# A two-layer mixer trunk on one core: the fourth Strassen sum of h built from the third by two transfers, two weight additions put ahead of the second of them, and the attended rows rounded together

## The chip, the cores and the metric

One Trainium2 chip, one of its cores. The metric is the device time of one execution in microseconds (us). TensorE multiplies matrices, ScalarE (ACT) and VectorE (DVE) do elementwise work, GpSimd (POOL) starts the transfers that add while they write, and SyncE (SP) starts the plain transfers of weights.

## The reference: what is computed

```python
for l in range(2):                                    # DEPTH = 2, x is 512 x 1024
    h = rms_norm(x, norm_g[l])
    proj = einsum('bsd,de->bse', h, w_in[l])          # columns: a_u a_v a_z b_q b_k b_v b_z i_q i_k i_w g_a g_b
    y_a = spatial_gating_branch(gelu(a_u), gelu(a_v), a_z, ...)
    att = sparse_attention_branch(q, k, v, qi, ki, i_w, topk=128)   # 4 heads x 128, keys chosen by an indexer
    y_b = att * silu(b_z)
    o_a = einsum('bse,ed->bsd', y_a, w_oa[l])
    o_b = einsum('bse,ed->bsd', y_b, w_ob[l])
    merged = sigmoid(g_a + gate_b[l, 0]) * o_a + sigmoid(g_b + gate_b[l, 1]) * o_b
    x = x + einsum('bsd,de->bse', merged, w_out[l])
```

All is float32.

## The kernel before

Every matrix product is made of three passes. Each operand is kept as a rounded part (`_hi`, type fp32r) and the rest (`_lo`), and three matmuls add hi times lo, lo times hi and hi times hi. ScalarE writes each hi (a Copy that rounds), VectorE each lo (a subtraction). A weight piece, a **unit**, is 256 rows by 512 columns (512 KB): it lands in one of four slots of `w_raw`, ScalarE rounds it (L1065), VectorE writes the rest (L1427), and the slot is free again.

The work of a layer is a fixed list of **jobs** on TensorE, in this order: iq, k, q, vb, va, u, zb, za (4 jobs each), ga (14), oa (8), gb (14), ob (8), out (14). Four jobs are called ZA0 to ZA3 here, and so on. Every engine walks through the same job numbers in a program written by hand. For job n ScalarE rounds the units that a table gives to n, empties the bank, and then does what stands "beside" the job: attention steps, sums. TensorE does an attention step (scores of step i, transposes of step i-1, weighted values of step i-2; L851, L842, L833) after ZA2 and then after GA0, GA2, GA4 and so on.

The ga, gb and out products use Strassen's scheme (in Winograd's form) on two by two blocks: seven products, each of two jobs, in the order a11 (GA0, GA1), a12 (GA2, GA3), s5 (GA4, GA5), s3 (GA6, GA7), s6 (GA8, GA9), s4 (GA10, GA11), a22 (GA12, GA13). Here a11, a12, a21 and a22 are the blocks of h transposed (upper or lower half of the channels, left or right half of the tokens), and the s are sums of them:

- s5 = a21 - a22, s3 = a21 - a22 - a11, s6 = a12 + a21 - a22 - a11, s4 = a21 - a11 (a sign apart).

The sums of h are made without VectorE: ScalarE copies one part into a buffer (`h_part_copied`, L1186), and POOL starts transfers that add further parts to it in place (`add_term`, L711). Each block has a hi and a lo part, so each is two terms. s5 is summed in `h5_raw`, s3 in `h3_raw`, s6 in `h6_raw`, and s4 in the lower token half of `g_a`, which is free only once the mixing matmuls before ZA1 are done; `h_beside` holds the lo part of -a11 meanwhile. `h_sum_rounded` (L1173) then rounds a sum on ScalarE, beside ZA3 (s5), GA0 (s3), GA2 (s6) and GA4 (s4), and `h_sum_remainder` (L1567) writes its rest on VectorE. Rounding s5 writes over a21, where it stood in h.

The weights of s5, s3, s4 and a22 are sums too. POOL adds a block of the weights to what a slot of `w_raw` still holds (`add_weights`, L737), once the rest of that slot's unit is written. In ga these are the units 4 and 5 (s5), 8 and 9 (s3), 10 and 11 (s4), 12 and 13 (a22). POOL issues all of it in the order of its program, and a wait there holds back what stands behind it. Units 6 and 7 (s6) are plain transfers by SP. ScalarE rounds units 4 and 5 at GA0, 6 and 7 at GA2, 8 at GA3, 9 at GA4, 10 at GA6.

After attention, `z_b` holds the attended rows times their gate, four heads of 128 channels. ScalarE rounds each to `yb_hi` (L1311), VectorE writes `yb_lo` (L1711), both at the jobs of `SPLIT_YB`. The first job of ob, OB0, uses them head by head. When all four are there, POOL reloads x into `x_sb` (L748), which the out jobs need.

Of the kernel before, what the change touches and what calls it, by code (L numbers as in the profile page):

```python
# [184 lines left out]
_slots = JOB_ZA[2:3] + JOB_GA[::2] + JOB_OA[::2] + JOB_GB[0:11:2]  # L185
AFTER_ATT = {_slots[i]: i for i in range(len(ATT_STEPS) + 2)}

SPLIT_YB = {JOB_GB[11]: [0, 1], JOB_GB[12]: [2], JOB_GB[13]: [3]}
assert min(SPLIT_YB) > max(AFTER_ATT)

X_AFTER = {2: [1], 4: [2], 5: [3]}

ROUNDS = TOPK // 8
H_PARTS = ["-a22 hi to s5", "-a22 lo beside", "a12 hi to s6", "-a11 hi to s3", "-a11 lo beside", "-a11 hi to s4"]
H_PARTS_AFTER = {JOB_VB[2]: 0, JOB_VB[3]: 1, JOB_VA[0]: 2, JOB_VA[1]: 3, JOB_VA[3]: 4, JOB_ZA[1]: 5}
H_TERMS = {"s5": 3, "s3": 2, "s6": 2, "s4": 3}
H_SIGN = {"s5": -1.0, "s3": 1.0, "s6": -1.0, "s4": -1.0}
H_HI_AFTER = {JOB_ZA[3]: "s5", JOB_GA[0]: "s3", JOB_GA[2]: "s6", JOB_GA[4]: "s4"}
H_LO_AFTER = {JOB_GA[1]: "s5", JOB_GA[3]: "s3", JOB_GA[5]: "s6", JOB_GA[7]: "s4"}
# [47 lines left out]
def trunk(nc, x, norm_g, w_in, gate_b, a_ln_g, a_ln_b, a_ws, a_bs, q_norm_g, k_norm_g, w_oa, w_ob, w_out,  # L247
          ident, rope_cs, out):
    ctx = ExitStack()
    with ctx:  # L250
# [298 lines left out]
        def top(tile, k=slice(0, HALF_K)):  # L549
            return tile[:, k, 0:SEQ // 2]  # L550

        def bottom(tile, k=slice(0, HALF_K)):
            return tile[:, k, SEQ // 2:SEQ]
# [89 lines left out]
        def _(pool):  # L643
# [6 lines left out]
            for layer in range(DEPTH):  # L650
# [56 lines left out]
                def add_term(name, n, src):  # L707

                    if n > 0:
                        pool.wait_ge(s_hterm[name].sem, s_hterm[name].at(layer, 16 * n))  # L710
                    pool.dma_start(h_sum_raw(name), src, accum_op=ALU.add).then_inc(s_hterm[name].sem, 16)  # L711

                def part_copied(part):
                    pool.wait_ge(s_hpart.sem, s_hpart.at(layer, H_PARTS.index(part) + 1))

# [10 lines left out]
                add_term("s3", 1, h_sum_raw("s5"))  # L726
                pool.wait_ge(s_hterm["s3"].sem, s_hterm["s3"].at(layer, 32))
                add_term("s6", 1, h_sum_raw("s3"))
                part_copied("-a11 hi to s4")
                add_term("s4", 0, h_beside[:])  # L730
                add_term("s4", 1, a21_hi)
                add_term("s4", 2, a21_lo)

                def add_weights(u):
                    slot = raw_slot(layer, u)
# [4 lines left out]
                for g in (GA_G, GB_G):  # L740
                    for u in range(UNIT_FIRST[g], UNIT_FIRST[g] + SEVEN):
                        if unit_adds(u):
                            add_weights(u)

                pool.wait_ge(s_yblo.sem, s_yblo.at(layer, HEADS))
                pool.wait_ge(s_stash.sem, s_stash.at(layer, 16))
# [304 lines left out]
        def _(act):  # L1051
# [108 lines left out]
            def h_sum_rounded(layer, name):  # L1160
                act.wait_ge(s_hterm[name].sem, s_hterm[name].at(layer, 16 * H_TERMS[name]))
                if name == "s5":
                    act.wait_ge(s_job.sem, s_job.at(layer, JOB_ZA[-1] + 1))
                    act.wait_ge(s_hterm["s4"].sem, s_hterm["s4"].at(layer, 48))
                    act.wait_ge(s_hterm["s3"].sem, s_hterm["s3"].at(layer, 32))
                if name == "s3":
                    act.wait_ge(s_hterm["s6"].sem, s_hterm["s6"].at(layer, 32))
                    act.wait_ge(s_hterm["s4"].sem, s_hterm["s4"].at(layer, 16))
                if name == "s6":
                    act.wait_ge(s_hslo.sem, s_hslo.at(layer, H_ROUNDED.index("s5") + 1))  # L1170
                if name == "s4":
                    act.wait_ge(s_ya.sem, s_ya.at(layer, A_GROUPS))
                nc.scalar.activation(gate_operand(name)[0], h_sum_raw(name), ACT.Copy,  # L1173
                                     scale=H_SIGN[name]).then_inc(s_hshi.sem, 1)

            def h_part_copied(layer, i):

                f, upper = (lambda block: block.bitcast(F32)), slice(HALF_K, KD)
                if H_PARTS[i] == "-a11 lo beside":
                    act.wait_ge(s_hterm["s5"].sem, s_hterm["s5"].at(layer, 16))  # L1180
                if H_PARTS[i] == "-a11 hi to s4":
                    act.wait_ge(s_mix.sem, s_mix.at(layer, A_GROUPS))
                dst, src, sign = [(h_sum_raw("s5"), f(bottom(h_hi, upper)), -1.0), (h_beside[:], f(bottom(h_lo, upper)), -1.0),
                                  (h_sum_raw("s6"), f(top(h_hi, upper)), 1.0), (h_sum_raw("s3"), f(top(h_hi)), -1.0),
                                  (h_beside[:], f(top(h_lo)), -1.0), (h_sum_raw("s4"), f(top(h_hi)), -1.0)][i]
                nc.scalar.activation(dst, src, ACT.Copy, scale=sign).then_inc(s_hpart.sem, 1)  # L1186

            def evacuate(layer, n):
# [79 lines left out]
            def beside(layer, n):  # L1268

                for i in AFTER_IDX.get(n, []):  # L1270
                    b, h = IDX_STEPS[i]
                    w = P * (b + 1)
                    act.wait_ge(s_idxp.sem, s_idxp.at(layer, i + 1))

                    if i >= 2:
                        act.wait_ge(s_idx.sem, s_idx.at(layer, i - 1))
                    nc.scalar.activation(probs[:, i % 2, 0:w], bank[3 + i % 2][:, 0:w], ACT.Relu).then_inc(s_relu.sem, 1)
                if n == AFTER_WS:
                    act.wait_ge(s_wst.sem, s_wst.at(layer, 1))
                    four = bank[5][:].rearrange("p (c q) -> p c q", c=A_GROUPS)  # L1280
                    act_.mark(nc.scalar.activation(ws_t[0:CHUNK], four[0:CHUNK], ACT.Copy))
                    act_.mark(nc.scalar.activation(ws_t[CHUNK:P, :, CHUNK:P], four[CHUNK:P, :, CHUNK:P], ACT.Copy))
                    act_.join(act)
                    act.sem_inc(s_wsc.sem, 1)
                if n - 1 in JOB_ZA:
                    c = n - 1 - JOB_ZA[0]
                    act.wait_ge(s_ya.sem, s_ya.at(layer, c + 1))
                    nc.scalar.activation(ya_hi[:, c], u_a[:, c], ACT.Copy).then_inc(s_yahi.sem, 1)
                if n in AFTER_ATT:
                    i = AFTER_ATT[n]  # L1290
                    if i >= 1 and i <= len(ATT_STEPS):
                        b = ATT_STEPS[i - 1][1]
                        w = P * (b + 1)
                        act.wait_ge(s_pt.sem, s_pt.at(layer, i))
                        if i >= 2:
                            act.wait_ge(s_pv.sem, s_pv.at(layer, i - 1))
                        nc.scalar.activation(probs_t[:, 0:w], bank[5][:, 0:w], ACT.Copy).then_inc(s_ptc.sem, 1)
                    if i < len(ATT_STEPS):
                        w = P * (ATT_STEPS[i][1] + 1)
                        act.wait_ge(s_max.sem, s_max.at(layer, i + 1))  # L1300
                        act_.mark(nc.scalar.activation(probs[:, i % 2, 0:w], probs[:, i % 2, 0:w], ACT.Exp,
                                                       bias=neg_max[:, i:i + 1], scale=ATT_SCALE,
                                                       accum_out=row_sum[:, i:i + 1]))
                        act_.join(act)
                        act.sem_inc(s_exp.sem, 1)
                        act.wait_ge(s_rowinv.sem, s_rowinv.at(layer, i + 1))
                        nc.scalar.activation(probs[:, i % 2, 0:w], probs[:, i % 2, 0:w], ACT.Copy,
                                             scale=row_inv[:, i:i + 1]).then_inc(s_prob.sem, 1)
                for h in SPLIT_YB.get(n, []):
                    act.wait_ge(s_yb.sem, s_yb.at(layer, TILES))  # L1310
                    nc.scalar.activation(yb_hi[:, h], z_b[:, h], ACT.Copy).then_inc(s_ybhi.sem, 1)  # L1311
                if n in H_PARTS_AFTER:
                    h_part_copied(layer, H_PARTS_AFTER[n])
                if n in H_HI_AFTER:
                    h_sum_rounded(layer, H_HI_AFTER[n])
                if n in JOB_OB:
                    d = n - JOB_OB[0]
                    if d == 0:
                        act.wait_ge(s_job.sem, s_job.at(layer, JOB_GB[-1] + 1))
                    if d == KD - 1:  # L1320
                        s5_rounded(layer, 0)
                        rounded(layer, OUT_U + 4)
                    if d % 2:
                        merged_hi(layer, d // 2)
                    if d == KD - 1:
                        s5_rounded(layer, 1)
                if n == JOB_OUT[2]:
                    sum_rounded(layer, "s6")
                if n == JOB_OUT[3]:
                    sum_rounded(layer, "s3")  # L1330
                if n == JOB_OUT[7]:
                    sum_rounded(layer, "s4")
                if n == JOB_OUT[8]:
                    bottom_hi(layer)
# [507 lines left out]
```

## Time and profile before

| what | value |
| --- | --- |
| time, median of 3 runs | 815.54 us (814.4 to 815.74) |
| time of the profiled execution | 814.92 us |
| its span | 813.1 us |
| TensorE busy | 776.1 us (95% of the span) |
| VectorE busy | 627.1 us (77%) |
| ScalarE busy | 429.0 us (53%) |
| POOL busy | 172.1 us (21%) |
| mean busy share of the DMA engines by POOL's queue, by SP's | 32.7%, 24.7% |

Busy time is time in which an engine executes something; start times are us from the start of the span. The span is 1.8 us shorter than the device time of the same execution. The two layers run one after the other: the first reaches GA0 at about 210 us, the second at about 608 us.

### The profile page before, as it was taken

To read this page: it belongs to the slowest core of one execution; us is meant where nothing else is said; L and a number is where in the kernel's file an instruction comes from. 1 tells how busy PE (TensorE), PEld (TensorE's weight loads), DVE (VectorE), ACT (ScalarE), POOL (GpSimd) and SP (SyncE) were. 2 spreads that over 40 slices of the span, in tenths; PEclk is the share of its full clock that TensorE was granted. 3 is DMA by queue.
4 is the path that set the end of the run, shared out by engine and by line. 5 is a ranking of instruction groups with operands and counts; after the bars stand their busy time and mean duration, and the time that the engine had idled before them with its cause. 6 is when DMAs were issued, how large, how long until landed. Compare 5 with 4: busy or idle time off the path is not lost.

```text
span 813.1 us, 12210 instructions
## 1 busy us (share of the span) xinstructions
PE 776.1 (95%) x4412; PEld 679.3 (84%) x4412; DVE 627.1 (77%) x1050; ACT 429.0 (53%) x790; POOL 172.1 (21%) x153
## 2 busy tenths in 40 slices
PE   7999999999769999999999999999994999999998
PEld 6988888888769889988899888888884998899886
DVE  5779999978278775669886899997962887746895
ACT  6576555343267546744564765544243764577242
POOL 1157501100220003012211664110012201110130
PEclk9999999999979999999999999999997999999999
DMA  9544237821976437676873531576247854476774
GB/s 335 201 128 132 61 112 165 199 60 53 165 120 159 127 79 130 184 212 136 185 230 104 168 107 61 128 163 177 79 91 116 133 178 78 96 123 197 207 135 125
DMA packets 55597, 114.72 MB, mean 141 GB/s; under 512 B 3568, under 2 KB 9904, under 8 KB 55536
## 3 DMA queue, kind: packets, MB, share of 16 engines
q0 software_dynamic: 24016, 48.32, 32.7%
q1 hardware_dynamic: 31232, 65.02, 24.7%
q8 instruction: 35, 0.57, 0.3%
q10 hardware_dynamic: 288, 0.59, 0.2%
q14 instruction: 26, 0.21, 0.1%
HBM read 97.14 MB, written 6.29 MB: 127 GB/s over the span
## 4 chain that ended last, share of the span: by engine, by line
PE 75%; DVE 9%; DMA 7%; issue 5%; ACT 3%; POOL 1%; ACTq 0%; DVEq 0%; SPq 0%; POOLq 0%
PE bank L859 15%; PE bank L861 15%; PE bank L860 15%; PE bank L980 4%; PE bank L927 4%; PE bank L929 4%; PE bank L928 4%; DVE w_lo L1427 3%; PE bank L833 2%; PE bank L896 2%; PE bank L898 2%; PE bank L897 2%; PE bank L851 2%; DMA g_a<-h_beside 2%; DMA g_a<-h_hi 1%
## 5 line engine op out<-in xcount | busy, mean ns | idle before, releaser
L1427 DVE TENSOR_TENSOR w_lo<-w_raw,w_hi 128x1024 fp32r<-128x1024 f32 x156 | 201.4, 1302 | 34.5 <-ACT w_hi L1065 30.5
L1065 ACT ACTIVATE w_hi<-w_raw 128x1024 fp32r<-128x1024 f32 x156 | 160.4, 1052 | 30.7 <-DMA w_raw<-in_w_out 16.6
L859 PE MATMUL bank<-w_lo,h_hi 128*128 128x512 f32 x256 | 100.5, 393 | 0.0
L861 PE MATMUL bank<-w_hi,h_hi 128*128 128x512 f32 x256 | 99.9, 390 | 0.0
L860 PE MATMUL bank<-w_hi,h_lo 128*128 128x512 f32 x256 | 99.8, 390 | 0.0
L927 PE MATMUL bank<-h_hi,w_lo 128*128 128x256 f32 x256 | 77.8, 304 | 2.0 <-DVEq L1581 2.0
L737 POOL DMA_DIRECT2D w_raw<-in_w_in x32 | 39.7, 1241 | 181.1 <-DVE w_lo L1427 173.7
L859 PE MATMUL bank<-h_lo,w_hi 128*128 128x512 f32 x192 | 75.2, 392 | 0.0
L861 PE MATMUL bank<-h_hi,w_hi 128*128 128x512 f32 x192 | 74.7, 389 | 0.0
L860 PE MATMUL bank<-h_hi,w_lo 128*128 128x512 f32 x192 | 74.7, 389 | 0.0
L928 PE MATMUL bank<-h_lo,w_hi 128*128 128x256 f32 x256 | 74.0, 289 | 0.0
L929 PE MATMUL bank<-h_hi,w_hi 128*128 128x256 f32 x256 | 73.9, 289 | 0.0
L927 PE MATMUL bank<-hs,w_lo 128*128 128x256 f32 x192 | 56.5, 294 | 2.7 <-DVE w_lo L1427 2.7
L1496 DVE MAX8 top<-score 128x8 f32<-128x256 f32 (+2 forms) x96 | 53.5, 558 | 5.5 <-DVE g_a L1629 2.6
L861 PEld LDWEIGHTS bank<-w_hi,h_hi 128*128 128x128 f32 x256 | 48.1, 188 | 10.3
L859 PEld LDWEIGHTS bank<-w_lo,h_hi 128*128 128x128 f32 x256 | 48.1, 188 | 9.3
L860 PEld LDWEIGHTS bank<-w_hi,h_lo 128*128 128x128 f32 x256 | 48.1, 188 | 9.3
L927 PEld LDWEIGHTS bank<-h_hi,w_lo 128*128 128x128 f32 x256 | 50.9, 199 | 4.1 <-DVEq L1581 2.4
L929 PE MATMUL bank<-hs,w_hi 128*128 128x256 f32 x192 | 53.8, 280 | 0.0
L928 PE MATMUL bank<-hs,w_hi 128*128 128x256 f32 x192 | 53.8, 280 | 0.0
L928 PEld LDWEIGHTS bank<-h_lo,w_hi 128*128 128x128 f32 x256 | 50.8, 199 | 1.6 <-issue 1.4
L1497 DVE MATCH_REPLACE8 score<-top,score 128x256 f32<-128x256 f32 (+2 forms) x96 | 52.1, 542 | 0.0
(209 smaller groups left out, 1862.7 us busy)
## 6 DMA issues: line engine op xcount, KB each, us to landing
w_raw<-in_w_in SPq DMA_DIRECT2D x88, 512.0 KB, 4.5
w_raw<-in_w_in POOLq DMA_DIRECT2D x32, 512.0 KB, 6.0
w_raw<-in_w_out POOLq DMA_DIRECT2D x16, 512.0 KB, 7.5
w_raw<-in_w_out SPq DMA_DIRECT2D x12, 512.0 KB, 4.1
out<-x_sb POOLq DMA_DIRECT2D x4, 1024.0 KB, 5.5
w_raw<-in_w_oa SPq DMA_DIRECT2D x8, 512.0 KB, 3.4
w_raw<-in_w_ob SPq DMA_DIRECT2D x8, 512.0 KB, 4.2
x_sb<-out POOLq DMA_DIRECT2D x2, 2048.0 KB, 8.9
```

The source lines that it names most:

```text
L737: pool.dma_start(w_raw[:, slot], block_weights(layer, u), accum_op=ALU.add) \
L859: nc.tensor.matmul(dst, s_h, m_l, start=(n == 0), stop=False)
L860: nc.tensor.matmul(dst, s_l, m_h, start=False, stop=False)
L861: last = nc.tensor.matmul(dst, s_h, m_h, start=False, stop=(n == len(pairs) - 1))
L927: nc.tensor.matmul(dst, w_lo[:, wk, col], a_hi[:, k], start=first and i == 0, stop=False, skip_group_check=True)
L928: nc.tensor.matmul(dst, w_hi[:, wk, col], a_lo[:, k], start=False, stop=False, skip_group_check=True)
L929: last = nc.tensor.matmul(dst, w_hi[:, wk, col], a_hi[:, k], start=False, stop=(k == HALF_K - 1), skip_group_check=True)
L980: last = nc.tensor.matmul(dst[:, 0:width], h[:, k, tok], w[:, k, first:first + width], start=(k == 0 and n == 0), stop=(k == KD - 1 and n ...
L1065: nc.scalar.activation(hi, w_raw[:, raw_slot(layer, u)], ACT.Copy).then_inc(s_whi.sem, 1)
L1427: nc.vector.tensor_tensor(lo, w_raw[:, raw_slot(layer, u)], hi.bitcast(F32), ALU.subtract) \
L1496: vec.link(dve, nc.vector.max(top8[:], s))
L1497: vec.link(dve, nc.vector.match_replace(s, top8[:], s, TAKEN))
```

## The change

s4 now starts from a22 (its hi part copied by ScalarE) and gets two terms: the finished sum s3 from `h3_raw`, and the lo part of a22. It had three, the lo part of -a11, and both parts of a21. The second term is started only after the weight additions of units 4 and 5. ScalarE, before it rounds s5, no longer waits for the terms of s4; before it rounds s3 it still waits for the first of them. And the attended rows are rounded at one place (GB11) in place of three, their rests are written at two places in place of three.

```diff
-SPLIT_YB = {JOB_GB[11]: [0, 1], JOB_GB[12]: [2], JOB_GB[13]: [3]}
+SPLIT_YB = {JOB_GB[11]: [0, 1], JOB_GB[12]: [2, 3]}
...
-H_PARTS = ["-a22 hi to s5", "-a22 lo beside", "a12 hi to s6", "-a11 hi to s3", "-a11 lo beside", "-a11 hi to s4"]
+H_PARTS = ["-a22 hi to s5", "-a22 lo beside", "a12 hi to s6", "-a11 hi to s3", "-a11 lo beside", "a22 hi to s4"]
...
-H_TERMS = {"s5": 3, "s3": 2, "s6": 2, "s4": 3}
+H_TERMS = {"s5": 3, "s3": 2, "s6": 2, "s4": 2}
...
-                part_copied("-a11 hi to s4")
-                add_term("s4", 0, h_beside[:])
-                add_term("s4", 1, a21_hi)
-                add_term("s4", 2, a21_lo)
+                part_copied("a22 hi to s4")
+                add_term("s4", 0, h_sum_raw("s3"))
...
                         if unit_adds(u):
                             add_weights(u)
+                        if u == UNIT_FIRST[GA_G] + 5:
+                            add_term("s4", 1, bottom(h_lo, slice(HALF_K, KD)).bitcast(F32))
...
                 if name == "s5":
                     act.wait_ge(s_job.sem, s_job.at(layer, JOB_ZA[-1] + 1))
-                    act.wait_ge(s_hterm["s4"].sem, s_hterm["s4"].at(layer, 48))
                     act.wait_ge(s_hterm["s3"].sem, s_hterm["s3"].at(layer, 32))
...
-                                  (h_beside[:], f(top(h_lo)), -1.0), (h_sum_raw("s4"), f(top(h_hi)), -1.0)][i]
+                                  (h_beside[:], f(top(h_lo)), -1.0), (h_sum_raw("s4"), f(bottom(h_hi, upper)), 1.0)][i]
...
-                for h in SPLIT_YB.get(n, []):
+                for h in range(HEADS if n == min(SPLIT_YB) else 0):
                     act.wait_ge(s_yb.sem, s_yb.at(layer, TILES))
                     nc.scalar.activation(yb_hi[:, h], z_b[:, h], ACT.Copy).then_inc(s_ybhi.sem, 1)
```

On POOL, this is the place of each layer between the sums of h and the weight additions of ga (`w_raw<-in_w_in` are those additions, the first two of them units 4 and 5; the sixteen are those of ga and gb):

```order
 L711 DMA h_raw<-h_lo 128x4x256
 L711 DMA h_raw<-h_raw 128x1024 x2
-L711 DMA g_a<-h_beside 128x4x256
-L711 DMA g_a<-h_hi 128x4x256
+L711 DMA g_a<-h_raw 128x4x256
+L735 DMA w_raw<-in_w_in 128x2x512 x2
 L711 DMA g_a<-h_lo 128x4x256
-L737 DMA w_raw<-in_w_in 128x2x512 x16
+L735 DMA w_raw<-in_w_in 128x2x512 x14
```

Units 4 and 5 stood behind three terms of s4 and now stand behind one; the last term has moved behind them, ahead of unit 8.

On ScalarE, this is the end of gb in the first layer, from the gates of GB10 on, before the change (L1134 are tanh of the gates, L1065 rounds weights):

```order
L1065 ACTIVATE w_hi<-w_raw 128x1024
L1134 ACTIVATE g_b<-g_b,gate_half 128x256 x2
L1311 ACTIVATE yb_hi<-z_b 128x512 x2
L1134 ACTIVATE g_b<-g_b,gate_half 128x256 x2
L1134 ACTIVATE g_b<-bank,gate_half 128x256 x2
L1311 ACTIVATE yb_hi<-z_b 128x512
L1134 ACTIVATE g_b<-bank,gate_half 128x256 x2
L1311 ACTIVATE yb_hi<-z_b 128x512
```

and of the changed kernel:

```order
L1065 ACTIVATE w_hi<-w_raw 128x1024
L1134 ACTIVATE g_b<-g_b,gate_half 128x256 x2
L1310 ACTIVATE yb_hi<-z_b 128x512 x4
L1134 ACTIVATE g_b<-g_b,gate_half 128x256 x2
L1134 ACTIVATE g_b<-bank,gate_half 128x256 x4
```

The third and the fourth rounding have moved ahead of the gates of s4 and a22.

## Rows read from the trace of the kernel before

**Rows 1.** Waits of TensorE by releaser: us in total, times, longest us.

```profile
PE bank L833 <- ACT probs_t L1297: 19.1, 2, 9.8
PE bank L842 <- ACT probs L1307: 2.7, 2, 1.4
...
PE bank L859 <- DVE yb_lo L1711: 1.0, 2, 0.5
```

**Rows 2.** Windows, first layer: length, busy (instructions) by engine, TensorE clock, DMA, GB/s.

```profile
209.80:218.90 9.10, 9.10 (x76) 8.91 (x74) 2.08 (x3) 1.12 (x2) 2.50 (x2) 1.00 0.83 117
218.90:228.20 9.30, 0.02 (x1) 0.00 (x0) 1.41 (x2) 4.34 (x6) 2.41 (x2) 0.62 0.83 128
...
230.90:234.70 3.80, 3.80 (x20) 3.80 (x20) 3.73 (x6) 2.90 (x5) 1.22 (x1) 0.50 0.39 47
234.70:242.90 8.20, 7.45 (x61) 7.18 (x60) 6.90 (x14) 6.02 (x12) 2.42 (x2) 1.00 0.99 154
```

**Rows 3.** Timeline of ScalarE: start us, us, line, what, [idle before <-releaser].

```profile
210.50 0.62 ACT L1288 ACTIVATE ya_hi<-u_a 128x512 fp32r<-128x512 f32 x1
219.84 1.06 ACT L1173 ACTIVATE h_hi<-h_raw 128x1024 fp32r<-128x1024 f32 x1 [8.72 <-DMA g_a<-h_lo]
222.37 1.06 ACT L1065 ACTIVATE w_hi<-w_raw 128x1024 fp32r<-128x1024 f32 x1 [1.47 <-DMA w_raw<-in_w_in]
225.93 1.06 ACT L1065 ACTIVATE w_hi<-w_raw 128x1024 fp32r<-128x1024 f32 x1 [2.50 <-DMA w_raw<-in_w_in]
...
227.88 0.27 ACT L1297 ACTIVATE probs_t<-bank 128x128 f32<-128x128 f32 x1
```

**Rows 4.** Timeline of POOL: when it issues its transfers.

```profile
201.27 1.31 POOL L711 DMA_DIRECT2D g_a<-h_beside  x1 [41.24 <-ACT g_a L1186]
...
213.77 1.28 POOL L711 DMA_DIRECT2D g_a<-h_lo  x1 [4.47 <-DMA g_a<-h_hi]
214.52 1.75 POOL L737 DMA_DIRECT2D w_raw<-in_w_in  x1
220.05 1.21 POOL L737 DMA_DIRECT2D w_raw<-in_w_in  x1 [3.78 <-issue]
```

**Rows 5.** The chain that ended last, two transfers: start us, us to landing.

```profile
201.27 6.22 DMA g_a<-h_beside
...
220.05 5.86 DMA w_raw<-in_w_in
```

**Rows 6.** Transfers issued at 214.52 us: KB, us to landing.

```profile
w_raw<-in_w_in POOLq DMA_DIRECT2D x1, 512.0 KB, 7.8
```

**Rows 7.** Timeline of VectorE, first layer.

```profile
229.79 1.21 DVE L1427 TENSOR_TENSOR w_lo<-w_raw,w_hi 128x1024 fp32r<-128x1024 f32 x1
...
232.42 1.22 DVE L1567 SCALAR_TENSOR_TENSOR h_lo<-h_raw,h_hi 128x1024 fp32r<-128x1024 f32 x1
...
241.61 1.22 DVE L1427 TENSOR_TENSOR w_lo<-w_raw,w_hi 128x1024 fp32r<-128x1024 f32 x1
```

**Rows 8.** Timeline of TensorE, the first matmul of GA6.

```profile
242.97 0.36 PE L927 MATMUL bank<-hs,w_lo 128*128 128x256 f32 x1 [0.82 <-DVE w_lo L1427]
```

**Rows 9.** Unit 8: when POOL issues it and ScalarE rounds it.

```profile
224.99 1.20 POOL L737 DMA_DIRECT2D w_raw<-in_w_in  x1 [3.74 <-DVE w_lo L1427]
```

```profile
238.29 1.04 ACT L1065 ACTIVATE w_hi<-w_raw 128x1024 fp32r<-128x1024 f32 x1
```

**Rows 10.** Second layer: the first term of s4 in the chain, and unit 5 on ScalarE.

```profile
599.59 6.21 DMA g_a<-h_beside
```

```profile
624.75 1.06 ACT L1065 ACTIVATE w_hi<-w_raw 128x1024 fp32r<-128x1024 f32 x1 [2.40 <-DMA w_raw<-in_w_in]
```

**Rows 11.** Timeline of ScalarE at the end of gb, first layer.

```profile
343.27 1.15 ACT L1311 ACTIVATE yb_hi<-z_b 128x512 fp32r<-128x512 f32 x2
...
351.29 0.63 ACT L1311 ACTIVATE yb_hi<-z_b 128x512 fp32r<-128x512 f32 x1 [0.19 <-ACT g_b L1134]
```

**Rows 12.** Timeline of TensorE in OB0, the fourth head's first product.

```profile
352.80 0.47 PE L859 MATMUL bank<-yb_lo,w_hi 128*128 128x512 f32 x1 [0.51 <-DVE yb_lo L1711]
```

More of the change, by code:

```diff
@@ L1180, in h_part_copied @@
                     act.wait_ge(s_hterm["s5"].sem, s_hterm["s5"].at(layer, 16))
-                if H_PARTS[i] == "-a11 hi to s4":
+                if H_PARTS[i] == "a22 hi to s4":
                     act.wait_ge(s_mix.sem, s_mix.at(layer, A_GROUPS))
```

## The prediction

> **What bounds the kernel now.** I read the waits of TensorE first, since it is busy 95% of the span and only its idle time or a slow clock can be won back quickly. The reader is to see that one line holds most of it: 19.1 us in two waits, for ScalarE's copy of the transposed probabilities, and 2.7 us more in two waits for the scaled probabilities [rows 1]. Next the windows around the first of these: TensorE ends GA2 at 218.9 us, stands until 228.2, and comes back at half its clock (0.50 granted, 1.2 of 2.4 GHz) until 234.7; three jobs took 9.10 us before that, so a ga job is 3.0 us [rows 2]. Third, ScalarE's timeline: it is idle too. It ends the third `ya_hi` at 211.12, then waits 8.72 us for the last term of s4 before it may round s5 at 219.84, then for unit 4 (222.37), then for unit 5 (225.93); only after those comes the copy that TensorE waits for, at 227.88 [rows 3]. Fourth, POOL: the three terms of s4 go out one after the other, each once the former has landed, at 201.27 and 213.77 for the first and the last, and units 4 and 5 queue behind them, at 214.52 and 220.05 [rows 4]. So the stall is made of two things in one line: a rounding (s5) that waits for a sum needed much later (s4, used at GA10), and two weight additions needed now (GA0 rounds them) that are issued behind that sum.
>
> From unit 5 on, the pace is VectorE's, not TensorE's: the rest of unit 5 is written at 229.79, that of s5 at 232.42, that of unit 8 at 241.61 [rows 7], and TensorE, though it came 9 us late and at half clock, waits again at 242.97 for that last one [rows 8]. So what this place can win is the time by which ScalarE gets unit 5 earlier. The slow clock is not a gain to be added: it lies inside the shadow of VectorE's chain.
>
> **The change, part by part.**
>
> *ScalarE's rounding of s5.* It no longer waits for s4. Its other conditions hold: TensorE ended ZA3 at 210, before the `ya_hi` of 210.50 [rows 3], s5 and s3 were complete before the part for s4 was copied, since POOL had only that part left to wait for at 201.27 [rows 4]. It starts where the third `ya_hi` ends, 211.1, and takes 1.06 [rows 3], so ScalarE can take unit 4 at 212.1 and unit 5 at 213.1 if they have landed.
>
> *POOL.* One transfer of 512 KB a layer is gone. The first term leaves at 201.27 as before and lands 6.22 us later, at 207.5 [rows 4, 5]; its source is another buffer of the same size, which I cost at nothing. Unit 4 may follow at 202.6, since its slot is free long before (POOL issued it right behind a term before too, at 214.52, with no idle time ahead [rows 4]). Two transfers in flight share the engines: the term issued at 213.77 had landed when ScalarE started at 219.84, unit 4 landed at 214.52 + 7.8 = 222.3, so 2.6 us behind, and unit 5 at 220.05 + 5.86 = 225.9, 3.6 us behind unit 4 [rows 3 to 6]. So unit 4 now lands at 210.1 to 211.1, ahead of 212.1. Unit 5 was issued 3.78 us after unit 4 with nothing shown that it waited for, and just as the term ahead of both had landed [rows 4]. I take it that the queue holds two of these and no third. Then unit 5 now leaves at about 207.8 and lands at 213.7 (5.86 later) if it runs as it did, or at 214.7 (3.6 behind unit 4) if the engines are shared. I take the middle, 214.2. ScalarE then has it 225.93 - 214.2 = **11.7 us** earlier. Upper bound: ScalarE's own 213.1, a gain of 12.8. Lower bound: 214.7 and the 0.5 us by which SP's units 6 and 7, in flight at the same time, might push it, a gain of 10.7.
>
> On transfers that add, a rule and the trace differ. The row gives 5.86 us for 512 KB [rows 5]. The Trainium skill, DMA: Bandwidth & Descriptors, section on the anatomy of one DMA on the GpSimd path, gives 2.0 us plus the bytes at 436 GB/s, an estimate of 3.2 us for this size. By it unit 5 would land at 211 and the gain would be the upper bound, 12.8. The trace does not agree, so the row decides.
>
> *The second layer.* From the first term to unit 5 on ScalarE it is 624.75 - 599.59 = 25.16 us, against 24.66 in the first [rows 3, 4, 10], with a first term that takes the same 6.21. The gain is 0.5 more: **12.2 us**, upper bound 13.3.
>
> *What is late next.* Everything that hung on unit 5 shifts by 11.7. The rest of s5 is done at 232.42 + 1.22 - 11.7 = 221.9; TensorE no longer stands after GA2 (the copy it wants comes at 227.88 - 11.7 = 216.2), does the attention step and GA3, and reaches GA4 at 222.2: no wait to speak of. It reaches GA6 two jobs and an attention step later, at 228.6, and the rest of unit 8 is there at 241.61 + 1.22 - 11.7 = 231.1. So the wait at GA6 grows from 0.82 [rows 8] to about 2.5 us. It is inside the 11.7: GA6 starts at 231.3 against 242.97.
>
> *The moved term.* The last term of s4 is issued behind unit 5 once there is room, about 211, and ahead of unit 8. It lands at about 218; s4 is rounded beside GA4, after unit 8, so not before 226. Unit 8 waits for the rest of unit 4 (about 214.3) and for room, leaves at about 214.5 and lands at 220.5 to 222. ScalarE wants it at 238.29 - 11.7 = 226.6 [rows 9]. So the moved term costs nothing, with 4.5 to 6 us in hand. Unit 9 is issued when the rest of unit 5 is written, which shifts with it.
>
> *ScalarE's copy for s4* reads another block of the same size: nothing.
>
> *The attended rows.* OB0 waited 0.51 us for the fourth head's rest [rows 12], because ScalarE rounded that head only behind the gates of a22, at 351.29 [rows 11]. Now the four roundings run from 343.27, two of them took 1.15, so the last ends at 345.6. That covers the gates of s4 by some 0.2 us, where ScalarE next waits for TensorE's a22, so nothing. The last rest is written at GB12, about 349, before OB0 wants it. A gain of 0.5 us a layer; the waits for it are 1.0 us in all [rows 1]: **1.0 us**. The reload of x starts some 4 us earlier and nothing waits for it before OUT0.
>
> **Sum.** 11.7 + 12.2 + 1.0 = 24.9 us. The profiled execution took 814.92 us (span 813.1), so it would take 790.0 (span 788.2). The median shown is 0.6 above it; I predict 790.6 for the median.
>
> **The rivals.**
>
> *Unit 5 is there before ScalarE asks.* If the pause of 3.78 us was no lack of room, three transfers run at 2.6 us apart: 207.5, 210.1, 212.7, before 213.1. Gains 12.8 + 13.3 + 1.0 = 27.1, time 788.4. Against it: the pause, in both layers. Chance 0.12. By the page DMA: Bandwidth & Descriptors of the Trainium skill (above) it would be the same time.
>
> *The transfers do not overlap here.* SP's units 6 and 7 run at the same time, and if unit 4 lands a whole 5.9 us behind the term and unit 5 another 5.9 behind that, it is 219.3, gains 6.6 + 7.1 + 1.0 = 14.7, time 800.8. Against it the 2.6 and 3.6 of the trace. Chance 0.07.
>
> *The clock.* The low clock took 7.1 us of the stall (a mean of 0.62 over 9.30 us) and lasted to 234.7, 13.6 us in all [rows 2]. Now TensorE has a wait of 2.5 us at GA6. Were the clock to fall on that, TensorE would work through such a stretch itself, at 0.19 us a matmul (3.80 us for 20) in place of 0.12 (9.10 us for 76): some 5 us a layer, time 801. Against it: after the 0.82 us wait the window shows 1.00. Chance 0.05. The Trainium skill, TensorE: Matmul & The Clock Gate, section on oscillation, tells of a kernel in which repeated waits for transfers kept the engine on the low clock; no row here shows that without a stall of 9 us.
>
> *Slower: the moved term holds unit 8.* POOL stands at the second term of s4 until the first has landed and there is room, and units 8 to 13 stand behind it. Past the 4.5 to 6 us in hand every us comes off the gain, and it decides at 11.7 + 6, some 18 us late: then the kernel is slower (each further 1 us costs 2, say 820 at 20 us late). Nothing in the trace takes 18 us. Chance 0.02. That something else holds ScalarE at the same place, so that nothing changes, has 0.02.
>
> **How the numbers follow.** Forecast 0.72, own range 789 to 793; ceiling 0.12 (788.4); no overlap 0.07 (800.8); clock 0.05 (801); slower 0.02; no change 0.02. A range of 787.5 to 797 takes the first two and partly overlapping or partly slowed cases. A change of 0.2%, 1.6 us, is about what can be told from none. Faster 0.96, same 0.02, slower 0.02.
>
> **What would show it.** TensorE's wait for `probs_t` (19.1 us) gone, and no low clock near 230 and 630. ScalarE rounding s5 at 211.1 without a wait, unit 4 at 212.1 without one, and unit 5 after about 1 us of waiting, at 214.2. POOL issuing at 201.3, 202.6, 207.8, then the term near 211. A wait of about 2.5 us at GA6 for `w_lo`. OB0 without a wait for `yb_lo`. Unit 8 not waited for by ScalarE. The prediction is wrong if unit 5 comes after 216, or if the low clock shows up again.

## The result, and the profile after

The changed kernel takes 793.58 us (median of 4 runs, 792.18 to 795.45) against 814.97 us before in the same comparison. The ratio is 0.9739, 95% interval 0.9715 to 0.9763: 21.4 us less, where 24.9 were forecast. The profiled execution took 792.18 us, span 790.4, and is the fastest of the four.

The waits of TensorE in the changed kernel (us in total, times, longest us), against [rows 1]:

```profile
PE bank L927 <- DVEq L1582: 3.6, 2, 1.8
PE bank L842 <- ACT probs L1306: 3.1, 2, 1.7
...
PE bank L927 <- DVEq L1580: 2.0, 2, 1.0
...
PE bank L927 <- DVE w_lo L1426: 1.4, 2, 0.8
```

The 19.1 us for `probs_t` are gone, and so is the wait for `yb_lo`. New is a wait of 1.8 us in each layer on something that VectorE released at L1582. ScalarE in the first layer, against [rows 3]:

```profile
210.33 1.05 ACT L1172 ACTIVATE h_hi<-h_raw 128x1024 fp32r<-128x1024 f32 x1
212.55 1.06 ACT L1065 ACTIVATE w_hi<-w_raw 128x1024 fp32r<-128x1024 f32 x1 [1.17 <-DMA w_raw<-in_w_in]
215.42 1.06 ACT L1065 ACTIVATE w_hi<-w_raw 128x1024 fp32r<-128x1024 f32 x1 [1.81 <-DMA w_raw<-in_w_in]
...
217.38 0.27 ACT L1296 ACTIVATE probs_t<-bank 128x128 f32<-128x128 f32 x1
```

It rounds s5 at once and then waits twice for weights, in all 3 us. POOL's issues, against [rows 4]:

```profile
200.59 1.31 POOL L711 DMA_DIRECT2D g_a<-h_raw  x1 [41.69 <-ACT g_a L1185]
201.34 3.03 POOL L735 DMA_DIRECT2D w_raw<-in_w_in  x2
207.38 1.30 POOL L711 DMA_DIRECT2D g_a<-h_lo  x1 [3.01 <-DMA g_a<-h_raw]
215.22 1.19 POOL L735 DMA_DIRECT2D w_raw<-in_w_in  x1 [6.54 <-DVE w_lo L1426]
```

Units 4 and 5 leave one right behind the other while the first term is in flight (x2, 201.34 to 204.37): there is no pause between them. Windows, to be read as [rows 2] (length, busy of TensorE, its weight loads, VectorE, ScalarE, POOL, then the clock):

```profile
209.10:218.20 9.10, 9.10 (x78) 9.08 (x76) 3.98 (x6) 5.35 (x8) 1.19 (x1) 1.00 1.15 218
...
222.20:226.00 3.80, 1.99 (x17) 1.78 (x16) 3.15 (x6) 1.33 (x3) 1.24 (x2) 1.00 0.86 134
226.00:230.00 4.00, 4.00 (x23) 4.00 (x22) 3.35 (x7) 3.55 (x8) 1.22 (x1) 0.57 0.95 140
230.00:234.00 4.00, 4.00 (x36) 4.00 (x36) 3.36 (x7) 3.37 (x9) 1.21 (x1) 1.00 0.81 130
```

The long low clock is gone. A short one stands in the first layer behind two waits, one of 1.4 us for `probs`, as before the change, and the new one of 1.8 us: 23 matmuls in 4 us in place of 36.

To compare kernels without the scatter at their start, I measure one stretch in each trace: from ScalarE's tanh of ZA3 (210.00 before, 209.32 after) to the end of the last wait of TensorE in ga, which every variant has. Before and after these are:

```profile
264.73 0.39 PE L927 MATMUL bank<-h_hi,w_lo 128*128 128x256 f32 x1 [0.99 <-DVEq L1581]
```

```profile
254.24 0.38 PE L927 MATMUL bank<-h_hi,w_lo 128*128 128x256 f32 x1 [0.98 <-DVEq L1580]
```

So the **ga stretch** of the first layer took 264.73 - 210.00 = 54.7 us before and 254.24 - 209.32 = 44.9 after: 9.8 us less. In the second layer it is 55.2 and 45.4: 9.8 again.

### The profile page after: what moved, and what is told of

It is laid out like the page before. It is cut to its first block, busy times and chain, and to the rows that moved or that the text cites. A ratio compares the mean times of both kernels' runs of the same rounds, so it can differ in the third digit from the quotient of the medians.

```text
span 790.4 us, 12206 instructions
## 1 busy us (share of the span) xinstructions
PE 772.4 (98%) x4412; PEld 677.4 (86%) x4412; DVE 626.6 (79%) x1050; ACT 428.4 (54%) x790; POOL 169.6 (21%) x151
## 4 chain that ended last, share of the span: by engine, by line
PE 83%; DVE 6%; DMA 5%; issue 2%; ACT 2%; POOL 0%; SPq 0%; DVEq 0%; ACTq 0%
PE bank L861 16%; PE bank L859 16%; PE bank L860 16%; PE bank L980 4%; DMA w_raw<-in_w_in 4%; PE bank L927 4%; PE bank L929 4%; PE bank L928 4%; PE bank L896 3%; PE bank L898 3%; PE bank L897 3%; DVE w_lo L1426 3%; PE bank L833 2%; PE bank L851 2%; PE bank L789 1%
## 5 line engine op out<-in xcount | busy, mean ns | idle before, releaser
L1065 ACT ACTIVATE w_hi<-w_raw 128x1024 fp32r<-128x1024 f32 x156 | 160.5, 1052 | 28.6 <-DMA w_raw<-in_w_out 15.4
```

Source lines behind the costliest of these rows:

```text
L1065: nc.scalar.activation(hi, w_raw[:, raw_slot(layer, u)], ACT.Copy).then_inc(s_whi.sem, 1)
```

## The experiments

Theory A is the prediction's: the time is set by when ScalarE gets unit 5. Theory B is the rival: only ScalarE's wait for s4 cost anything, and the order on POOL does not matter. Each ratio is to the kernel before in the same comparison: 814.97 us for the changed kernel, 815.17 for e1 to e4, 814.53 for e5 to e7, 814.84 for e8 and e9; these three groups ran on three chips. A difference between kernels of two such groups can be off by some tenths for that. The last column is when ScalarE starts on unit 5, behind its tanh of ZA3; where its row shows units 4 and 5 as x2, unit 5 starts 1.06 us before the row's end.

| kernel | median us | ratio to before (95%) | ga stretch, first layer | unit 5 behind ZA3's tanh |
| --- | --- | --- | --- | --- |
| before | 814.97 | 1 | 54.7 | 15.9 |
| changed | 793.58 | 0.9739 (0.9715 to 0.9763) | 44.9 | 6.1 |
| e1, both terms first | 799.72 | 0.9818 (0.9803 to 0.9833) | 48.9 | 10.1 |
| e2, ScalarE waits for s4 | 803.18 | 0.9855 (0.9841 to 0.987) | 50.3 | 11.5 |
| e7, kernel before with units 4, 5 first | 806.25 | 0.9894 (0.9881 to 0.9908) | 50.7 | 11.9 |
| e3, changed with units 4, 5 first | 786.03 | 0.9642 (0.9626 to 0.9658) | 41.7 | 2.9 |
| e4, changed with units 6, 7 late | 786.45 | 0.9649 (0.9635 to 0.9663) | 41.7 | 2.9 |
| e9, e3 and e4 together | 786.24 | 0.9649 (0.9635 to 0.9664) | 41.7 | 2.9 |
| e8, e3 with top-k rounds moved | 784.93 | 0.9631 (0.9615 to 0.9647) | 40.5 | 2.9 |
| e5, kernel before with the rows alone | 812.73 | 0.998 (0.9971 to 0.9989) | | |
| e6, changed without the rows | 794.55 | 0.9757 (0.9744 to 0.977) | | |

The two columns differ by 38.8 us in every row but that of e8 (37.6): however unit 5 was brought forward or held back, by the wait, by the order or by SP's transfers, the end of the ga stretch moved with it, us for us. This is theory A in one number.

**e1, the order on POOL undone.**

```diff
                 add_term("s4", 0, h_sum_raw("s3"))
+                add_term("s4", 1, bottom(h_lo, slice(HALF_K, KD)).bitcast(F32))
...
-                        if u == UNIT_FIRST[GA_G] + 5:
-                            add_term("s4", 1, bottom(h_lo, slice(HALF_K, KD)).bitcast(F32))
```

> The changed kernel with both terms of s4 ahead of the additions of units 4 and 5 on POOL. Theory A (unit 5's landing sets the time, as predicted): the second term can leave only when the first has landed (207), so units 4 and 5 land behind it, at about 215 and 218 instead of 212.5 and 215.4. ScalarE takes unit 5 about 3 us later in each layer, so the time is 5 to 7 us above the changed kernel, some 799 us. Theory B (all that cost was ScalarE's wait for s4 before rounding s5, the order on POOL is immaterial): no change against the changed kernel, 793.5 us.

It is 6.1 us above the changed kernel. ScalarE's timeline:

```profile
210.78 1.05 ACT L1171 ACTIVATE h_hi<-h_raw 128x1024 fp32r<-128x1024 f32 x1
216.45 1.06 ACT L1064 ACTIVATE w_hi<-w_raw 128x1024 fp32r<-128x1024 f32 x1 [4.62 <-DMA w_raw<-in_w_in]
219.89 1.06 ACT L1064 ACTIVATE w_hi<-w_raw 128x1024 fp32r<-128x1024 f32 x1 [2.38 <-DMA w_raw<-in_w_in]
```

s5 is rounded at once and it still waits, now 7 us for the weights. Unit 5 comes at 219.89 - 209.77 = 10.1 us behind ZA3's tanh, against 215.42 - 209.32 = 6.1 in the changed kernel. Theory B would have had no difference, and falls.

**e2, ScalarE's wait put back.**

```diff
                     act.wait_ge(s_job.sem, s_job.at(layer, JOB_ZA[-1] + 1))
+                    act.wait_ge(s_hterm["s4"].sem, s_hterm["s4"].at(layer, 32))
```

> The changed kernel with one wait put back: ScalarE rounds s5 only when s4 is complete. Theory A: s4's second term lands at 218.9, s5 is rounded at 219.0, units 4 and 5, which have long landed, at 220 and 221; unit 5 is taken 5.6 us later in each layer, the time is about 11 us above the changed kernel, 804 to 805 us. Theory B: the whole gain is lost, 814 to 815 us.

It loses 9.6 us of the 21.4.

```profile
219.62 1.06 ACT L1173 ACTIVATE h_hi<-h_raw 128x1024 fp32r<-128x1024 f32 x1 [8.45 <-DMA g_a<-h_lo]
220.58 1.99 ACT L1065 ACTIVATE w_hi<-w_raw 128x1024 fp32r<-128x1024 f32 x2
```

The old wait is back at nearly its old length, but units 4 and 5 (x2) are there and follow without a gap: unit 5 at 221.5 in place of 225.93 [rows 3].

**e7, the order alone, on the kernel before.** Units 4 and 5 are added ahead of the three terms of s4; ScalarE's wait stays.

```diff
+                for u in (UNIT_FIRST[GA_G] + 4, UNIT_FIRST[GA_G] + 5):
+                    add_weights(u)
                 part_copied("-a11 hi to s4")
                 add_term("s4", 0, h_beside[:])
...
-                        if unit_adds(u):
+                        if unit_adds(u) and u > UNIT_FIRST[GA_G] + 5:
                             add_weights(u)
```

> The kernel before with one edit: units 4 and 5 are added ahead of the three terms of s4, ScalarE's wait for s4 stays. Theory A: s5 is rounded at 219.8 as before or up to 1 us earlier, then units 4 and 5, long landed, at 220.9 and 221.9 instead of 222.4 and 225.9: 4 us in each layer, the time 8 us below before, 807 us. Theory B (only the wait for s4 costs): no change, 815 us.

8.3 us below before (814.53 in its comparison), as theory A has it. TensorE still waits, 11.0 us in place of 19.1:

```profile
PE bank L835 <- ACT probs_t L1299: 11.0, 2, 5.7
```

**e3, units 4 and 5 ahead of everything in the changed kernel.** The same edit as in e7, in front of `part_copied("a22 hi to s4")`, and both terms of s4 behind it.

> The changed kernel with the additions of units 4 and 5 moved ahead of both terms of s4, so that POOL issues them while it would stand idle (from about 195 us). Theory A: both have landed before ScalarE asks, unit 5 is taken at 212.3 instead of 215.4, 3.1 us earlier in each layer; the waits of TensorE at the attention step after GA2 (1.4) and at GA4 (1.8) vanish. Time 6 us below the changed kernel, 787 to 788 us. Theory B: no change. A third theory C (VectorE's chain behind unit 5 has no use for it, because TensorE or another chain is the pace by then): under 2 us less.

7.5 us below the changed kernel. POOL's and ScalarE's timelines:

```profile
193.15 1.21 POOL L732 DMA_DIRECT2D w_raw<-in_w_in  x1 [31.96 <-DVE w_lo L1427]
200.28 1.23 POOL L732 DMA_DIRECT2D w_raw<-in_w_in  x1 [5.92 <-DVE w_lo L1427]
202.86 1.31 POOL L711 DMA_DIRECT2D g_a<-h_raw  x1 [1.36 <-ACT g_a L1186]
209.41 1.28 POOL L711 DMA_DIRECT2D g_a<-h_lo  x1 [5.24 <-DMA g_a<-h_raw]
```

```profile
212.42 1.05 ACT L1173 ACTIVATE h_hi<-h_raw 128x1024 fp32r<-128x1024 f32 x1
213.37 1.99 ACT L1066 ACTIVATE w_hi<-w_raw 128x1024 fp32r<-128x1024 f32 x2
```

POOL stood idle for 32 us before the first of them, until its slot was free; the second had to wait for its own slot until 200.28, and both still landed before ScalarE asked. ScalarE goes through s5, unit 4 and unit 5 without a wait. The ga stretch falls by 3.2 us, the 3.1 expected. Of TensorE's waits of 1.4 and 1.8 us the first is gone, and of the second 0.2 is left:

```profile
PE bank L928 <- DVEq L1583: 0.4, 2, 0.2
```

**e4, SP's units 6 and 7 held back.** The forecast had unit 5 at 12.9 us after the first term's issue, the trace 215.42 - 200.59 = 14.8. I suspected the two plain transfers that run at the same time.

```diff
                     slot = raw_slot(layer, u)
+                    if g == GA_G and qt == 6:
+                        sem, value = landed(layer, u - 1)
+                        sp.wait_ge(sem, value)
```

> The changed kernel with SP's plain transfers of units 6 and 7 held until unit 5 has landed. Theory D (these two share the engines with the first term and units 4 and 5, and pushed unit 5 from the predicted 213.5 to 215.4): unit 5 is taken 1.5 to 2.6 us earlier in each layer, time 3 to 5 us lower, if units 6 and 7 (asked for at 221) still come in time. If the missing 1.9 us has another cause, unit 5 stays at 215.4 and the time at 793.5 us.

7.1 us below the changed kernel, more than expected. SP starts units 6 and 7 when unit 5 has landed, so its row tells when that was:

```profile
201.38 1.31 POOL L714 DMA_DIRECT2D g_a<-h_raw  x1 [41.55 <-ACT g_a L1188]
202.14 3.03 POOL L738 DMA_DIRECT2D w_raw<-in_w_in  x2
```

```profile
212.65 1.37 SPq L634 DMA_DIRECT2D w_raw<-in_w_in  x2
```

```profile
212.08 1.99 ACT L1068 ACTIVATE w_hi<-w_raw 128x1024 fp32r<-128x1024 f32 x2
```

Unit 5 landed 212.65 - 201.38 = 11.3 us after the first term's issue, 3.5 us sooner than with the two beside it, and ScalarE takes both units without a wait (in the second layer it waits 0.27 us for unit 5). Most of the delay fell on unit 4. The transfer issued at 201.34 in the changed kernel and the one at 202.14 in e4, us to landing:

```profile
w_raw<-in_w_in POOLq DMA_DIRECT2D x1, 512.0 KB, 11.2
```

```profile
w_raw<-in_w_in POOLq DMA_DIRECT2D x1, 512.0 KB, 7.9
```

In the changed kernel the two plain transfers themselves took 6.4 and 9.9 us:

```profile
w_raw<-in_w_in SPq DMA_DIRECT2D x1, 512.0 KB, 6.4
```

```profile
w_raw<-in_w_in SPq DMA_DIRECT2D x1, 512.0 KB, 9.9
```

Before the change they took 5.7 and 5.9 us at this place, where POOL had one transfer that adds in flight at a time in place of three.

**e9, both.**

> e3 and e4 together: units 4 and 5 added first, and SP's units 6 and 7 held until unit 5 has landed. Each alone already has unit 5 landed before ScalarE asks. If that is the limit of this lever, the two together give what one gives, 785.5 to 786.5 us; if each took away a different wait, the sum shows, 780 us or less.

No further gain: 786.24 us and the same ga stretch of 41.7. Once unit 5 has landed before ScalarE asks, nothing more is to be had from its landing.

**e8, top-k rounds moved.** On e3, so that the landing of unit 5 is out of the way.

```diff
-               23: [(2, 1), (3, 1)], 24: [(3, 1)], 25: [(3, 1)], 33: [(3, 1)], 35: [(3, 1)], 37: [(3, 1)], 39: [(3, 1)],
-               41: [(3, 1)], 43: [(3, 1)], 45: [(3, 1)], 47: [(3, 2)], 49: [(3, 1)], 51: [(3, 2)], 53: [(3, 1)]}
+               23: [(2, 1), (3, 1)], 24: [(3, 1)], 25: [(3, 1)], 39: [(3, 1)],
+               41: [(3, 1)], 43: [(3, 1)], 45: [(3, 2)], 47: [(3, 2)], 49: [(3, 2)], 51: [(3, 2)], 53: [(3, 2)]}
```

> e3 (units 4 and 5 ahead of both terms of s4) with three of VectorE's top-k rounds for the last block (each a MAX8 and a MATCH_REPLACE8, 1.4 us) taken out of GA1, GA3 and GA5 and done in oa and gb instead. If VectorE's chain from unit 5 to GA10 sets the pace, as the prediction says, each round taken out brings the rests of units 8 and 9 forward: TensorE's waits at GA6 and later in ga (0.8 + 0.6 + 1.0 us a layer) go, 3 to 5 us in all, some 782 us. If TensorE itself is the pace by now, nothing changes (786 us).

1.1 us, not 3 to 5; the two intervals against before (0.9615 to 0.9647 and 0.9626 to 0.9658) overlap, so in the times it is not sure. In the traces the ga stretch is 1.2 us shorter. The waits of TensorE:

```profile
PE bank L928 <- DVEq L1581: 1.9, 2, 1.0
PE bank L928 <- DVE w_lo L1427: 1.9, 2, 0.9
```

In e3 they were 1.9 and 2.7. By the edit the three rounds go to GA13, OA3 and OA7, none to gb; GA13 stands behind the end of the stretch. Taking 4.2 us of VectorE's work out of the stretch shortened it by 1.2: I had over-read VectorE's share of the pace. The trace shows what stands behind the wait of 0.9 that stays, the one for the rest of unit 9:

```profile
230.14 0.16 DVE L1504 RECIPROCAL row_inv<-row_sum 128x1 f32<-128x1 f32 x1 [1.83 <-ACTq L1305]
230.22 1.21 DVE L1427 TENSOR_TENSOR w_lo<-w_raw,w_hi 128x1024 fp32r<-128x1024 f32 x1
```

VectorE itself stood idle for 1.83 us just before that rest, for row sums of the attention step that ScalarE makes behind its rounding of unit 9 and its gates. In e3 the same wait was 0.61. With less to do, VectorE waits for ScalarE; no run moved ScalarE's part.

**e5 and e6, the attended rows**, alone on the kernel before, and undone in the changed one:

```diff
-SPLIT_YB = {JOB_GB[11]: [0, 1], JOB_GB[12]: [2], JOB_GB[13]: [3]}
+SPLIT_YB = {JOB_GB[11]: [0, 1], JOB_GB[12]: [2, 3]}
...
-                for h in SPLIT_YB.get(n, []):
+                for h in range(HEADS if n == min(SPLIT_YB) else 0):
```

> The kernel before with only the attended rows rounded in one go. As predicted: OB0's wait of 0.51 us for the fourth head's rest goes in each layer, 1.0 us less (ratio 0.9988) and no wait for yb_lo in the profile. Rival: the four roundings ahead of the gates of s4 and a22 delay a bank of ob, and the time stays or rises.

> The changed kernel with the rounding of the attended rows as before, in three places. As predicted: OB0 waits about 0.5 us again in each layer, the time is 1.0 us above the changed kernel, some 794.6 us. Rival: no difference.

Alone it gives 1.8 us (0.9 to 2.4 by its interval); undone, the medians are 1.0 us apart (1.5 by the ratios), with overlapping intervals. In e6 the wait is back, and it is absent in e5:

```profile
PE bank L859 <- DVE yb_lo L1710: 1.0, 2, 0.5
```

The forecast of 1.0 us is inside both. The traces are sharper. From the first matmul of OB0 to the last that reads `yb_lo`, in the kernel before:

```profile
350.06 0.40 PE L859 MATMUL bank<-yb_lo,w_hi 128*128 128x512 f32 x1
399.39 0.39 PE L897 MATMUL bank<-w_hi,yb_lo 128*128 128x512 f32 x1
```

and in e5:

```profile
349.96 0.40 PE L859 MATMUL bank<-yb_lo,w_hi 128*128 128x512 f32 x1
398.49 0.39 PE L897 MATMUL bank<-w_hi,yb_lo 128*128 128x512 f32 x1
```

That is 49.33 us against 48.53, and 49.32 (e6) against 48.54 (changed); the second layer has the same 0.8. So the rows are worth 1.6 us in all. The listed wait of 0.51 us understates its cost: here matmuls start 0.23 us apart while each is 0.39 long, and the one that waited started 0.90 us behind the one before it.

## Why the prediction was right, step by step

**The stall and its two causes** were right. By the runs, of the 21.4 us the wait of ScalarE accounts for 9.6 when it is put back (e2), and the order on POOL for 6.1 when it is undone (e1). Each alone leaves the other, as the weights and the sum both stood ahead of the copy that TensorE waited for. On the kernel before, the order alone gave 8.3 (e7). The two numbers do not add up to the whole, as both the wait and the order act on one time, that of unit 5. What the dropped third term is worth by itself was not tried: no kernel keeps the wait and the old order with two terms.

**The size of the gain in ga was too large**: forecast 11.7 and 12.2, measured 9.8 and 9.8. Both lie below my lower bound of 10.7. The term that was off is the landing of unit 5, 14.8 us after the first term's issue in place of 12.9. I took 0.5 us as the most by which SP's units 6 and 7 might push it, a size that no row showed; e4 shows that they pushed it by 3.5, nearly all of it at unit 4, which landed some 5.4 us behind the first term (at 212.55) where I had 2.6 to 3.6. I had also taken a pause of 3.78 us [rows 4] for a queue that holds no third transfer. The changed kernel issues three without a pause, so that reading fell, and without SP's transfers unit 5 would have landed at 11.3 us after the first term, sooner than the forecast of 12.9. One error partly hid the other, which was luck. What the pause before was is open; in e1, too, two additions go out behind a term without it. In the second layer unit 5 was later still, 602.84 - 587.50 = 15.3 us behind the first term's issue:

```profile
587.50 1.29 POOL L711 DMA_DIRECT2D g_a<-h_raw  x1 [42.10 <-ACT g_a L1185]
```

```profile
602.84 1.06 ACT L1065 ACTIVATE w_hi<-w_raw 128x1024 fp32r<-128x1024 f32 x1 [1.84 <-DMA w_raw<-in_w_in]
```

So the 0.5 us that I added for this layer was there after the change too, and was no gain. The median of 793.58 us lies inside the range of 787.5 to 797, by its part for partly overlapping transfers, and outside the 789 to 793 that I had called the forecast's own.

**The rival of no overlap** (800.8 us) came true in part: it named the right cause, SP's units, and unit 4 did land 5.4 us behind the term (it had 5.9), but unit 5 then only 2.9 behind unit 4. The ceiling rival (788.4), in which unit 5 is there before ScalarE asks, is what e3 and e4 show, at 786.0 and 786.5 us. In e4 the three landed at 207.5, 210.0 and 212.65, which is this rival's 207.5, 210.1, 212.7.

**What is late next** was placed wrongly. I expected no wait at GA4 and 2.5 us at GA6. TensorE waited 1.40 us in the attention step after GA2, as before the change, and 1.81 at GA4:

```profile
225.10 0.39 PE L927 MATMUL bank<-h_hi,w_lo 128*128 128x256 f32 x1 [1.81 <-DVEq L1582]
```

L1582 is the line after VectorE's addition for a12 out of a bank. GA4 opens a bank, and this one is free only when VectorE has added what GA2 left in it, at

```profile
224.21 0.68 DVE L1579 TENSOR_TENSOR g_a<-g_a,bank 128x512 f32<-128x512 f32 x1
```

which stands in VectorE's program behind the rest of unit 5, a top-k round, and the rests of s5 and of unit 6. I had looked only at the operands of GA4 (s5's rest was done at 223.2). It changed where the time went, not the sum, since all of it hangs on unit 5: that came 9.8 us earlier behind ZA3's tanh, and the stretch is 9.8 shorter, in both layers.

**The moved term** held back nothing behind it: it was issued at 207.38 in place of the expected 211, and unit 8 at 215.22, once the rest of unit 4 was written, with ScalarE not waiting for it. From 207.38 it was in flight together with unit 5; whether that cost unit 5 anything is not shown, as e4 has it too.

**The clock.** The long low stretch went, as forecast. But the prediction had named a low clock that shows up again as a sign of being wrong, and by its letter that sign came; the other sign, unit 5 after 216, was just missed (215.42). A short one appeared in the first layer after the two waits (0.57 over 4 us), not in the second, and both layers gained the same 9.8 us in ga. In the second, TensorE waited at GA6 for `w_lo`, both waits of the 1.4 us in the first answer above; in the first, slowed down, it came there without a wait. So the slow stretch took the place of a wait, which speaks for the chain behind unit 5 as the pace up to GA6. From ScalarE's start on unit 5 to the end of that wait it is 242.97 - 225.93 = 17.0 us before, and 17.1 in e1, e2, e3 and e4. By e8 this chain is ScalarE's as well as VectorE's. The rival had given a low clock 0.05 and 5 us a layer; it came small and cost nothing measurable.

**The rest.** Ga gave 19.6 us and the attended rows 1.6 in the traces, where 1.0 was forecast: together 21.2. That agrees with the measured 21.4 without a further cause.

## What to carry to other kernels

When an engine waits in program order for a sum that is used much later, look not only at that wait but at what the same slow queue does behind it: here the wait and the order of the queue each held a part of one stall, and each could be measured alone. Before accepting an order, look for the time in which the queue is idle: POOL had been idle for 32 us just before (e3: another 7.5 us for moving two weight additions). To see what one event is worth, measure from it to a later fixed point in every variant: here unit 5 to the last wait in ga was 38.8 us in all but one. Count every transfer in flight at the place, on other queues too, before trusting a duration that was measured without them.

## What the runs showed of the hardware

In this kernel transfers that add into SBUF landed later with plain ones beside them: three of 512 KB on POOL's queue took 11.3 us from the first issue to the last landing with no plain ones beside them (e4), and 14.8, until ScalarE took the last, with two plain ones of 512 KB from SP (changed kernel; the second term of s4 follows the three in both), which in turn took 6.4 and 9.9 us in place of 5.7 and 5.9.
